# Four neighbouring rows of a down matrix on each partition, and eight passes of 64 columns in place of two transposes

## The chip, the core and the metric

The kernel runs on one core of a Trainium2 chip. The metric is the device time of one execution in microseconds (us); lower is better. Weights and activations are float32 and come from HBM through the core's 16 DMA engines into SBUF. TensorE (PE) multiplies into PSUM; its weight loads are shown as an engine of their own, PEld. ScalarE (ACT) and VectorE (DVE) read PSUM, SyncE (SP) issues nearly all transfers.

## What is computed

Two layers of a transformer trunk over 256 tokens of width 1024. Each layer has a mixture of three kinds of attention and then a mixture of 32 experts, of which every token takes two. The part that the change touches is the expert:

```python
def expert_block(args):
    xb, e = args
    h = jax.nn.silu(xb @ w_gate[e]) * (xb @ w_up[e])
    return h @ w_down[e]
```

`w_gate[e]` and `w_up[e]` are 1024 x 512, `w_down[e]` is 512 x 1024: 2 MB each in float32, so 6.29 MB for an expert and 403 MB for the 64 experts of both layers.

## The kernel before, in words

Each engine runs a program of its own, and semaphores join them. The experts' matrices come as chunks of 2 MB, always in the order gate, up, down, through a ring of eight slots in SBUF and, for two of the first chunks of a layer, through two extra places. SP issues a chunk as soon as its slot is free (L431 for gate and up, L429 for down); TensorE frees slots by raising a semaphore (L1570). While a layer's attention runs, the first ten chunks of its experts are fetched; then the DMA stands until TensorE frees the slots of the first expert. A layer has four rounds of eight experts.

An expert has at most 32 tokens in the regular pass, and on TensorE it takes these steps:

- `products` (L1521): the 32 gathered token columns times gate and up. The four halves (gate 0:256, gate 256:512, up 0:256, up 256:512) are computed side by side in four column tiles of 32 columns, so that `gu_ps` has four groups of 32 rows by 256 columns. ACT copies that to `h_rows`, and then TensorE frees the two slots.
- `turned` / `turns` (L1530 and L1532): `h_rows` is transposed back into `h_ps`, so that hidden units lie on the partitions. This is two transposes of 128 x 128 (L1530). Two more transposes (L1532) turn the gates and places of the tokens into `pgt_ps`.
- `neg_exp` on ACT (L668) and `hidden` on DVE (L1044 to L1047) make silu(gate) * up, which is `hid`.
- `down_of` (L1538): `hid` times the down chunk, in four column tiles of 32 columns, one for each `k` of the chunk.
- `add` (L1546): the result is scattered into the accumulators of all tokens.

The order on TensorE, for expert e, is products(e), down_of(e - 1), turned(e), add(e - 1). At the end of a round it is down_of(6), products(7), turned(7), add(6), down_of(7), add(7).

Which hidden unit sits on which partition is set twice, and the two must agree: by the view of the down matrix that SP loads (`down_v`), and by which columns of `h_rows` a transpose takes (`by_step`). Before, partition p holds units 2p, 2p + 1, 256 + 2p and 257 + 2p: two runs of two rows, 8 KB each.

Of the kernel before, what the change touches and what calls it, by code (L numbers as in the profile page):

```python
# [20 lines left out]
ALU = mybir.AluOpType  # L21
# [145 lines left out]
def trunk(nc, x_d, w_in, w_out, norm_mix, norm_ffn, rel_bias, lam_q1, lam_k1, lam_q2, lam_k2,  # L167
# [4 lines left out]
    with ctx:  # L172
# [14 lines left out]

        h_ps = pv[:, 1, 0:2 * P].rearrange("p (c h s) -> p c h s", c=HALF // P, h=4)
        pgt_ps = pv[:, 1, 2 * P:(2 + TOK) * P]
# [77 lines left out]

        hid = take(2 * P).rearrange("p (b c h s) -> p b c h s", b=2, c=HALF // P, h=2)
        e_neg = take(2 * P).rearrange("p (b c n) -> p b c n", b=2, c=HALF // P)
        sig = take(P).rearrange("p (c n) -> p c n", c=HALF // P)  # L270
        rlog = take(TOK * R_COLS).rearrange("p (t n) -> p t n", t=TOK)
# [14 lines left out]

        ident = con[:, C_ID:C_ID + P]

        xT_raw = rows.rearrange("p t f -> p (t f)").rearrange("p (j s) -> p j s", j=KD)
# [53 lines left out]
        up_v = w_up.rearrange("l e (p j) d -> (l e) p j d", j=KD)  # L343
        down_v = w_down.rearrange("l e (h p c) n -> (l e) p h c n", h=2, c=KE // 2)

# [4 lines left out]
        def down_chunk(flat):  # L350
            return flat.rearrange("p (k n) -> p k n", k=KE)

        def down_rows(flat):

            return flat.rearrange("p (h c n) -> p h c n", h=2, c=KE // 2)

# [32 lines left out]
        def _(sp):  # L389
# [6 lines left out]
            for l in range(DEPTH):  # L396
# [14 lines left out]
                for m in range(ROUNDS):  # L411
                    for c in (*range(6), *EXTRA, 6, 7, *range(EXTRA[-1] + 1, 3 * BODY)) if m == 0 else range(3 * BODY):
                        e = l * N_EXPERTS + m * BODY + c // 3
                        if m == 0 and c == 5:
                            sp.wait_ge(lg_done, at(l, NS, 8))
                            sp.dma_start(gain_ffn, bcast_row(norm_ffn, l, D_MODEL)).then_inc(gain_f_in, 16)
                        if m == 0 and c in EXTRA:
                            i = EXTRA.index(c)
                            sp.wait_ge(ssq_ready, l * RMS + 5)
                            if c % 3 == 2:  # L420
                                sp.dma_start(down_rows(extra[i]), down_v[e]).then_inc(extra_full[i], 16)
                            else:
                                sp.dma_start(extra[i].rearrange("p (j n) -> p j n", j=KD), (gate_v, up_v)[c % 3][e]
                                             ).then_inc(extra_full[i], 16)
                            continue
                        s, fill = place(m * 3 * BODY + c)
                        sp.wait_ge(slot_free[s], at(l, FILLS[s], fill))
                        if c % 3 == 2:
                            sp.dma_start(down_rows(ring[:, s, :]), down_v[e]).then_inc(slot_full[s], 16)  # L429
                        else:  # L430
                            sp.dma_start(chunk(s, 512), (gate_v, up_v)[c % 3][e]).then_inc(slot_full[s], 16)  # L431
                    if m == 0 and l + 1 < DEPTH:
                        load_small(sp, l + 1)
# [5 lines left out]
                with sp.If(more > 0):  # L439
                    with sp.Fori(0, more) as k:  # L440
                        i = done + k
                        e = sp.value_load(over_e_i[0:1, bass.ds(k, 1)], min_val=0, max_val=N_EXPERTS - 1)
                        for c, w in enumerate((gate_v, up_v, down_v)):
                            sp.wait_ge(slot_free[c], at(l, FILLS[c], FILLS[c] + 1))
                            sp.wait_ge(over_free, i + 1)
                            sp.sem_inc(passed["sp"], 1)
                            sp.dma_start(down_rows(ring[:, c, :]) if c == 2 else chunk(c, 512), w[l * N_EXPERTS + e]
                                         ).then_inc(over_full[c], 16)
# [59 lines left out]
        def _(act):  # L508
# [30 lines left out]
            for l in range(DEPTH):  # L539
# [127 lines left out]
                def neg_exp(b):  # L667
                    return nc.scalar.activation(e_neg[:, b], h_ps[:, :, 0:2, :].rearrange("p c h s -> p c (h s)"),  # L668
                                                ACT.Exp, scale=-1.0)
# [66 lines left out]
        def _(dve):  # L736
# [11 lines left out]
            for l in range(DEPTH):  # L748
# [292 lines left out]
                def hidden(b, ready, turned):  # L1041

                    gate, up = (h_ps[:, :, a:a + 2, :].rearrange("p c h s -> p c (h s)") for a in (0, 2))
                    own.link(v.tensor_scalar(sig, e_neg[:, b], 1.0, None, ALU.add))  # L1044
                    own.link(v.reciprocal(sig, sig))  # L1045
                    own.link(v.tensor_tensor(sig, gate, sig, ALU.mult))
                    v.tensor_tensor(hid[:, b].rearrange("p c h s -> p c (h s)"), up, sig, ALU.mult  # L1047
                                    ).then_inc(ready, 1)
# [106 lines left out]
        def _(pe):  # L1155
# [6 lines left out]
            for l in range(DEPTH):  # L1162
# [363 lines left out]
                def turns(i):  # L1526

                    by_step = h_rows.rearrange("q (p c) -> q c p", c=HALF // P)
                    for c in range(HALF // P):
                        turn_(h_ps[:, c].rearrange("p h s -> p (h s)"), by_step[:, c], ident)  # L1530
                    for t in range(TOK):
# [3 lines left out]
                def down(flat, b, half):  # L1535

                    for k in range(KE):
                        ins = mm(tr[k * CAP:(k + 1) * CAP, half], hid[:, b, k % 2, k // 2, :],  # L1538
                                 down_chunk(flat)[:, k, 512 * half:512 * half + 512],
# [163 lines left out]
```

## Time and profile before

| what | value |
|---|---|
| median of 3 runs | 1256.07 us (1255.79 to 1257.69) |
| the profiled execution | 1253.63 us |
| its span, first to last instruction | 1251.3 us |
| TensorE busy | 85% of the span |
| TensorE weight loads busy | 49% |
| VectorE, ScalarE, GpSimd busy | 28%, 19%, 2% |
| read from HBM | 441.59 MB, 354 GB/s over the span |
| mean granted TensorE clock | 0.927 |

The profile is of one execution. Busy shares are means over a span of very different stages: in two long stretches the DMA moves some 425 GB/s without a pause, and between them it does less than half of that. So the views by stage and the chain of work that ended last say more than the shares. A line number stands for a line of the kernel; a helper's line can stand for many calls. Matmuls are pipelined, so the start to start distance of neighbours says more than the duration of one.

### The profile page before, as it was taken

How to read it: one execution, taken by the hardware profiler on the slowest of the kernel's cores; microseconds unless marked ns; L12 is line 12 of the kernel's file. 1: busy time of each engine (PE TensorE's matmuls, PEld its weight loads, DVE VectorE, ACT ScalarE, POOL GpSimd, SP SyncE). 2: the span in 40 equal slices, each digit the busy share in tenths (PEclk: the TensorE clock that was granted, in tenths of full speed). 3: DMA queues.
4: the chain of work that ended last, by engine and by line, in shares of the span. 5: the costliest groups of instructions: out<-in, count | busy, mean ns of one | idle time of the engine just before them, and what ended most of it. 6: DMA issues, size and time to landing. Idle time of an engine off the chain costs nothing.

```text
span 1251.3 us, 18635 instructions
## 1 busy us (share of the span) xinstructions
PE 1060.1 (85%) x7940; PEld 608.6 (49%) x7940; DVE 345.5 (28%) x962; ACT 237.3 (19%) x574; POOL 18.8 (2%) x49
## 2 busy tenths in 40 slices
PE   8999999976877788777799999998787878696876
PEld 4877565443433344434358765554444344343532
DVE  3444562211211111111235364721111211111113
ACT  2234212201111111111112341121111111110111
POOL 1000100000000000000010000000000000000000
PEclk9999999987989888888999999999889888897989
DMA  7674549999999999999995144699999999999994
GB/s 259 247 305 172 212 150 426 425 359 426 427 425 421 425 426 425 426 425 426 412 387 210 53 176 178 257 428 426 425 425 426 424 425 423 426 425 427 425 424 181
DMA packets 63141, 443.89 MB, mean 355 GB/s; under 512 B 10409, under 2 KB 14929, under 8 KB 30289
## 3 DMA queue, kind: packets, MB, share of 16 engines
q1 hardware_dynamic: 61072, 440.94, 85.7%
q10 hardware_dynamic: 1984, 1.72, 0.4%
q8 instruction: 66, 1.08, 0.3%
q14 instruction: 19, 0.15, 0.0%
HBM read 441.59 MB, written 1.06 MB: 354 GB/s over the span
## 4 chain that ended last, share of the span: by engine, by line
DMA 46%; PE 44%; SPq 2%; ACT 2%; DVE 2%; issue 2%; PEld 1%; PEldq 0%; POOL 0%; POOLq 0%; ACTq 0%; DVEq 0%
DMA ring<-in_w_up 45%; PE pv L1521 14%; PE pj L1194 7%; PE pj L1200 4%; PE pj L1428 4%; PE tr L1538 3%; SPq L383 2%; PE pj L1546 2%; PE lg L1546 2%; ACT arena L511 1%; PE tr L1507 1%; PE lg L1229 1%; DMA ring<-in_w_in 1%; DMA bias<-bias_lines 1%; PE pv L1260 1%
## 5 line engine op out<-in xcount | busy, mean ns | idle before, releaser
L1521 PE MATMUL pv<-ring,xT 128*32 128x256 f32 x4032 | 298.4, 457 | 159.2 <-DMA ring<-in_w_up 159.1
L1521 PEld LDWEIGHTS pv<-ring,xT 128*32 128x32 f32 x4032 | 167.8, 131 | 292.2 <-issue 245.1
L1044 DVE TENSOR_SCALAR arena<-arena 128x128 f32<-128x128 f32 x64 | 14.5, 227 | 705.6 <-ACT arena L668 705.3
L1546 PE MATMUL pj<-arena 128*128 128x512 f32 x256 | 131.5, 596 | 0.0
L1546 PE MATMUL lg<-arena 128*128 128x512 f32 x256 | 130.8, 592 | 0.0
L511 ACT ACTIVATE arena<-pv 128x256 f32<-128x256 f32 x64 | 24.5, 383 | 542.2 <-PE pv L1521 542.2
L1538 PE MATMUL tr<-ring,arena 128*32 128x512 f32 x992 | 118.7, 594 | 0.0
L511 ACT ACTIVATE arena<-tr 128x512 f32<-128x512 f32 (+3 forms) x168 | 92.3, 558 | 126.8 <-PE tr L1538 106.5
L1194 PE MATMUL pj<-xT,ring 128*128 128x256 f32 (+1 forms) x480 | 107.9, 381 | 0.6 <-PE pj L1194 0.6
L1194 PEld LDWEIGHTS pj<-xT,ring 128*128 128x128 f32 (+1 forms) x480 | 87.3, 185 | 17.5 <-issue 2.7
L1546 PEld LDWEIGHTS lg<-arena 128*128 128x128 f32 x256 | 48.7, 190 | 61.2 <-issue 61.2
L1507 PEld LDWEIGHTS tr<-arena,rows 128*128 128x128 f32 x512 | 59.7, 192 | 7.0 <-issue 6.7
L1546 PEld LDWEIGHTS pj<-arena 128*128 128x128 f32 x256 | 43.7, 191 | 37.3 <-issue 37.3
L1045 DVE RECIPROCAL arena<-arena 128x128 f32<-128x128 f32 x64 | 61.0, 952 | 2.2
L1507 PE MATMUL tr<-arena,rows 128*128 128x128 f32 x512 | 59.7, 275 | 0.0
L1538 PEld LDWEIGHTS tr<-ring,arena 128*32 128x32 f32 x992 | 32.8, 110 | 54.9 <-issue 48.1
L1428 PE MATMUL pj<-ring,xT 128*128 128x512 f32 x128 | 57.4, 596 | 1.0 <-ACT xT L511 1.0
L1530 PEld LDWEIGHTS pv<-con,arena 128*128 128x128 f32 x128 | 20.2, 207 | 59.4 <-issue 59.4
L511 ACT ACTIVATE xT<-tr 128x512 f32<-128x512 f32 x36 | 21.3, 597 | 109.9 <-PE tr L1507 90.0
L1530 PE MATMUL pv<-con,arena 128*128 128x128 f32 x128 | 31.9, 331 | 11.9 <-ACT arena L511 11.9
L511 ACT ACTIVATE arena<-pj 64x256 f32<-64x256 f32 (+2 forms) x52 | 22.2, 428 | 77.0 <-PE pj L1194 63.9
L1428 PEld LDWEIGHTS pj<-ring,xT 128*128 128x128 f32 x128 | 23.4, 190 | 26.9 <-issue 26.9
(200 smaller groups left out, 753.4 us busy)
## 6 DMA issues: line engine op xcount, KB each, us to landing
ring<-in_w_up SPq DMA_DIRECT2D x64, 2048.0 KB, 21.8
ring<-in_w_gate SPq DMA_DIRECT2D x62, 2048.0 KB, 30.8
ring<-in_w_down SPq DMA_DIRECT2D x62, 2048.0 KB, 26.3
ring<-in_w_in SPq DMA_DIRECT2D x10, 2048.0 KB, 19.5
ring<-in_w_out SPq DMA_DIRECT2D x4, 2048.0 KB, 16.9
arena<-in_w_down SPq DMA_DIRECT2D x2, 2048.0 KB, 7.9
arena<-in_w_gate SPq DMA_DIRECT2D x2, 2048.0 KB, 12.3
ring<-in_w_in SPq DMA_DIRECT2D x2, 1760.0 KB, 14.4
```

What stands on the lines that cost most here:

```text
L383: eng.dma_start(dst, src).then_inc(small_in, 16)
L511: return nc.scalar.activation(out, in_, ACT.Copy, **k)
L1044: own.link(v.tensor_scalar(sig, e_neg[:, b], 1.0, None, ALU.add))
L1045: own.link(v.reciprocal(sig, sig))
L1194: ins = mm(out, w[:, j], xT[:, j, :], start=(j == 0), stop=(j == KD - 1))
L1200: ins = mm(out, src[:, j, t * P:(t + 1) * P], chunk(i, n)[:, j, c:c + m], start=(j == 0), stop=(j == KD - 1))
L1428: ins = mm(pj[:, half], xT[:, k, t * P:(t + 1) * P], chunk(6 + half, 512)[:, k, :], start=(k == 0), stop=(k == KD - 1))
L1507: ins = mm(wide_ps[:, j * n:(j + 1) * n], rows[:, t, j * P:(j + 1) * P], pick[:, t, 0:n], start=(t == 0), stop=(t == TOK - 1))
L1521: ins = mm(gu_ps[i * CAP:(i + 1) * CAP, :], xg[:, q, j, c:c + CAP], w[:, j, :], start=(j == 0), stop=(j == KD - 1), tile_position=(0, i * ...
L1530: turn_(h_ps[:, c].rearrange("p h s -> p (h s)"), by_step[:, c], ident)
L1538: ins = mm(tr[k * CAP:(k + 1) * CAP, half], hid[:, b, k % 2, k // 2, :], down_chunk(flat)[:, k, 512 * half:512 * half + 512], start=True, ...
L1546: ins = mm(acc[t][half], pgT[:, b, t, :], y[:, 512 * half:512 * half + 512], start=False, stop=last, skip_group_check=True)
```

## The change

The down chunk gets the layout that gate and up have: partition p holds the rows 4p to 4p + 3 of the matrix, 16 KB in one run. To match that, the halves of the hidden units go to halves of the partitions: units 0:256 to partitions 0 to 63, units 256:512 to partitions 64 to 127. `turns` takes every fourth column of `h_rows` (64 of them) as the stationary side and half of the identity's columns (64) as the moving side; with four steps `c` and two halves `h` there are eight passes, and the column tile (0, 64h) puts the result in the lower or upper partitions. They are ordinary float32 matmuls and no longer transposes. `neg_exp` and `hidden` read the new order, with as many elements as before.

```diff
-        h_ps = pv[:, 1, 0:2 * P].rearrange("p (c h s) -> p c h s", c=HALF // P, h=4)
+        h_ps = pv[:, 1, 0:2 * P].rearrange("p (c g s) -> p c g s", c=KE, g=2)
...
-        hid = take(2 * P).rearrange("p (b c h s) -> p b c h s", b=2, c=HALF // P, h=2)
+        hid = take(2 * P).rearrange("p (b c s) -> p b c s", b=2, c=KE)
...
+        ident_by_half = ident.rearrange("p (g h s) -> p g h s", g=2, h=2)
...
-        down_v = w_down.rearrange("l e (h p c) n -> (l e) p h c n", h=2, c=KE // 2)
+        down_v = w_down.rearrange("l e (p c) n -> (l e) p c n", c=KE)
...
-                            sp.dma_start(down_rows(ring[:, s, :]), down_v[e]).then_inc(slot_full[s], 16)
+                            sp.dma_start(down_chunk(ring[:, s, :]), down_v[e]).then_inc(slot_full[s], 16)
...
-                    return nc.scalar.activation(e_neg[:, b], h_ps[:, :, 0:2, :].rearrange("p c h s -> p c (h s)"),
+                    return nc.scalar.activation(e_neg[:, b], h_ps[:, :, 0, :],
                                                 ACT.Exp, scale=-1.0)
...
-                    gate, up = (h_ps[:, :, a:a + 2, :].rearrange("p c h s -> p c (h s)") for a in (0, 2))
+                    gate, up = h_ps[:, :, 0, :], h_ps[:, :, 1, :]
...
-                    by_step = h_rows.rearrange("q (p c) -> q c p", c=HALF // P)
-                    for c in range(HALF // P):
-                        turn_(h_ps[:, c].rearrange("p h s -> p (h s)"), by_step[:, c], ident)
+                    by_step = h_rows.rearrange("q (p c) -> q c p", c=KE)
+                    for c in range(KE):
+                        for h in range(2):
+                            mm(h_ps[64 * h:64 * h + 64, c], by_step[:, c], ident_by_half[:, :, h, :],
+                               start=True, stop=True, tile_position=(0, 64 * h), skip_group_check=True)
...
-                        ins = mm(tr[k * CAP:(k + 1) * CAP, half], hid[:, b, k % 2, k // 2, :],
+                        ins = mm(tr[k * CAP:(k + 1) * CAP, half], hid[:, b, k, :],
```

## Rows read from the trace of the kernel before

**Rows 1.** The page's first part: each engine's busy time, share of span, instructions.

```profile
PE 1060.1 (85%) x7940; PEld 608.6 (49%) x7940; DVE 345.5 (28%) x962; ACT 237.3 (19%) x574; POOL 18.8 (2%) x49
```

**Rows 2.** The page's chain that ended last, shares of the span by line.

```profile
DMA ring<-in_w_up 45%; PE pv L1521 14%; PE pj L1194 7%; PE pj L1200 4%; PE pj L1428 4%; PE tr L1538 3%; SPq L383 2%; PE pj L1546 2%; PE lg L1546 2%; ACT arena L511 1%; PE tr L1507 1%; PE lg L1229 1%; DMA ring<-in_w_in 1%; DMA bias<-bias_lines 1%; PE pv L1260 1%
```

**Rows 3.** Windows of both expert stages: length, engines, PE clock, DMA share, GB/s.

```profile
265.00:606.00 341.00, 260.07 (x2240) 137.63 (x2240) 54.02 (x125) 47.37 (x99) 0.00 (x0) 0.87 1.01 425
822.00:1216.00 394.00, 316.84 (x2738) 167.88 (x2741) 67.44 (x155) 58.43 (x122) 0.00 (x0) 0.89 1.01 425
```

**Rows 4.** The chain by time, layer 0 (start, us, what): transfers of up.

```profile
383.17 24.73 DMA ring<-in_w_up
...
415.57 23.40 DMA ring<-in_w_up
...
448.15 20.29 DMA ring<-in_w_up
...
476.41 21.58 DMA ring<-in_w_up
```

**Rows 5.** The same chain in layer 1.

```profile
909.06 20.47 DMA ring<-in_w_up
937.50 22.67 DMA ring<-in_w_up
```

**Rows 6.** DMA view, 377.95 to 380.80 us: packets, MB, share of 16 engines.

```profile
q1 hardware_dynamic: 144, 1.18, 99.2%
```

**Rows 7.** DMA view, 368.20 to 375.80 us; 16 of the packets are semaphore writes.

```profile
q1 hardware_dynamic: 208, 3.15, 97.6%
```

**Rows 8.** The DMA view of 265 to 606 us, all packets and the queue.

```profile
DMA packets 12891, 144.95 MB, mean 425 GB/s; under 512 B 1102, under 2 KB 1102, under 8 KB 1102
...
q1 hardware_dynamic: 12871, 144.64, 100.5%
```

**Rows 9.** The page's DMA queues: the one that brings instructions.

```profile
q8 instruction: 66, 1.08, 0.3%
```

**Rows 10.** Windows where the experts of layer 1 begin, columns as in rows 3.

```profile
798.00:802.00 4.00, 3.94 (x68) 2.14 (x66) 3.59 (x10) 0.60 (x1) 0.00 (x0) 1.00 0.02 6
802.00:806.00 4.00, 3.31 (x56) 2.15 (x60) 3.51 (x14) 0.66 (x2) 0.00 (x0) 1.00 0.65 188
```

**Rows 11.** Timeline of SP in the same place: start, us, engine, line, transfer.

```profile
802.51 0.33 SPq L431 DMA_DIRECT2D ring<-in_w_up  x1
...
809.48 0.33 SPq L431 DMA_DIRECT2D ring<-in_w_gate  x1
```

**Rows 12.** A window in layer 0, while the next layer's small tensors are loaded.

```profile
260.00:264.00 4.00, 4.00 (x16) 1.43 (x18) 3.31 (x8) 0.18 (x1) 0.00 (x0) 1.00 0.68 152
```

**Rows 13.** Timeline of the last expert of layer 1, after its products.

```profile
1234.80 0.29 DVE L1047 TENSOR_TENSOR arena<-pv,arena 128x128 f32<-128x128 f32 x1
...
1236.25 0.64 PE L1538 MATMUL tr<-ring,arena 128*32 128x512 f32 x4
```

**Rows 14.** Timeline of TensorE around the four transposes of one expert.

```profile
1219.99 0.50 PE L1530 MATMUL pv<-con,arena 128*128 128x128 f32 x2
1220.33 0.38 PE L1532 MATMUL pv<-con,arena 128*128 128x128 f32 x2
1220.55 0.59 PE L1546 MATMUL pj<-arena 128*128 128x512 f32 x1
```

**Rows 15.** Timeline of TensorE from a full-width matmul to column tiles of 32.

```profile
1223.55 0.59 PE L1546 MATMUL lg<-arena 128*128 128x512 f32 x1
1224.07 0.16 PEld L1538 LDWEIGHTS tr<-ring,arena 128*32 128x32 f32 x8 [0.76 <-issue]
```

**Rows 16.** Timeline of TensorE: sixteen matmuls of 64 columns in attention.

```profile
729.78 2.00 PE L1260 MATMUL pv<-arena 128*128 128x64 f32 x16
```

**Rows 17.** Timeline of TensorE: one expert's products at full clock.

```profile
1227.78 3.66 PE L1521 MATMUL pv<-ring,xT 128*32 128x256 f32 x64 [1.78 <-DMA ring<-in_w_up]
```

More of the change, by code:

```diff
@@ L266, in trunk @@
         pgT = take(2 * TOK * P).rearrange("p (b t s) -> p b t s", b=2, t=TOK)
-        hid = take(2 * P).rearrange("p (b c h s) -> p b c h s", b=2, c=HALF // P, h=2)
-        e_neg = take(2 * P).rearrange("p (b c n) -> p b c n", b=2, c=HALF // P)
-        sig = take(P).rearrange("p (c n) -> p c n", c=HALF // P)
+        hid = take(2 * P).rearrange("p (b c s) -> p b c s", b=2, c=KE)
+        e_neg = take(2 * P).rearrange("p (b c s) -> p b c s", b=2, c=KE)
+        sig = take(P).rearrange("p (c s) -> p c s", c=KE)
         rlog = take(TOK * R_COLS).rearrange("p (t n) -> p t n", t=TOK)
@@ L351, in down_chunk @@
             return flat.rearrange("p (k n) -> p k n", k=KE)
-        def down_rows(flat):
-            return flat.rearrange("p (h c n) -> p h c n", h=2, c=KE // 2)
         def nk(t):
@@ L420, in _ @@
                             if c % 3 == 2:
-                                sp.dma_start(down_rows(extra[i]), down_v[e]).then_inc(extra_full[i], 16)
+                                sp.dma_start(down_chunk(extra[i]), down_v[e]).then_inc(extra_full[i], 16)
                             else:
@@ L446, in _ @@
                             sp.sem_inc(passed["sp"], 1)
-                            sp.dma_start(down_rows(ring[:, c, :]) if c == 2 else chunk(c, 512), w[l * N_EXPERTS + e]
+                            sp.dma_start(down_chunk(ring[:, c, :]) if c == 2 else chunk(c, 512), w[l * N_EXPERTS + e]
                                          ).then_inc(over_full[c], 16)
@@ L1046, in hidden @@
                     own.link(v.tensor_tensor(sig, gate, sig, ALU.mult))
-                    v.tensor_tensor(hid[:, b].rearrange("p c h s -> p c (h s)"), up, sig, ALU.mult
+                    v.tensor_tensor(hid[:, b], up, sig, ALU.mult
                                     ).then_inc(ready, 1)
```

## The prediction, made before the changed kernel was run

> **What bounds the kernel now.** The busy shares point to TensorE, 85% busy [rows 1], but they are a mean over unlike stages. The chain of work that ended last gives 45% of the span to one transfer, that of the up chunks [rows 2]. The windows over the expert stages say why: the DMA is busy all the time (share 1.01) at 425 GB/s in both layers, while TensorE is busy for 260 of 341 us and for 317 of 394 us, at a mean granted clock below full [rows 3]. The chain in order of time shows the beat. Two experts lie between neighbouring pieces, and a piece ends when its up chunk has landed: 407.90, 438.97, 468.44 and 497.99 us [rows 4]. The usual distance is 29.5 us, 14.76 us an expert, in which TensorE stands 3 us (77 us over 26.7 experts in layer 1, 81 over 23.1 in layer 0 [rows 3]). So inside these stretches only what the DMA does counts. A layer's stretch begins when TensorE frees its first slots and ends when the last up chunk has landed. Then the end is TensorE's own: turned(7), add(6), down_of(7), add(7).
>
> **Part 1: the down chunk in runs of 16 KB.** A window that holds only down packets has 144 of 8 KB; 99.2% of 16 engines for 2.85 us is 45.2 us, 314 ns each [rows 6]. A window with only gate and up has 192 packets of 16 KB and 16 semaphore writes; 97.6% of 16 engines for 7.6 us is 118.7 us, 617 ns each [rows 7]. The long stretch agrees: 144.64 MB in 11,769 large packets means 5,887 of 16 KB and 5,882 of 8 KB, and 1.005 x 16 x 341 us over them is 931 ns for one of each [rows 8]. So 16 KB cost 628 ns in two pieces and 617 in one. These durations overlap a little: 16 of either kind for each engine and expert make 14.90 us where the beat is 14.76, so each packet hides about 4 ns, and the gain of a joined pair is 7 to 11 ns. With 8 pairs for each engine and chunk, a down chunk gets 0.055 to 0.09 us shorter. I take 0.07. Which chunks count? In layer 1 the DMA stands at 798 to 802 us (share 0.02) [rows 10] and restarts with the up chunk of expert 3, issued at 802.51 [rows 11]. From there to the last up chunk, that of expert 31, the down chunks of experts 3 to 30 pass: 28. Layer 0 has the same order. 2 x 28 x 0.07 = 3.9 us gained (bounds 3.1 to 5.0; nothing, if the fixed part of a packet is paid elsewhere).
>
> **A page that gives less.** The Trainium skill, page "DMA: Bandwidth & Descriptors", section "Why small descriptors are slow (HBM only)", gives each packet about 3 beats of 32 bytes and each operation 32 bytes of metadata. By that one 8 KB packet fewer would save 4 of some 520 beats, 0.8% of 628 ns, an estimate of 5 ns; the gain would be about 2.2 us in place of 3.9. The rows show 7 to 11 ns, so I keep them.
>
> **Part 2: the small loads in layer 0.** Between 260 and 264 us the DMA is busy only 0.68 of the time, because SP has been issuing the next layer's small tensors [rows 12]; 1.3 us are empty. A down chunk with half as many descriptors may let SP get through sooner, or not. Bounds 0 and 1.3 us gained; I take 0.3.
>
> **Part 3: the turns on TensorE.** Before, two transposes and two more follow one another at about 0.11 us: from 1220.33 to 1220.55 is one such pair, and the first pair needs 0.34 from its start because the array comes from tiles of 32 columns [rows 14]. So the pair that goes is worth 0.22 us. What comes is eight float32 matmuls. The trace shows a float32 matmul as two weight loads and two matmuls (64 records at L1521 for the 32 calls of one expert [rows 17]) and a transpose as one (two for two calls [rows 14]), so it is 16 pairs of 64 columns. No row has such a tile. The nearest: sixteen full-width matmuls of 64 columns take 2.00 us, 0.111 from start to start [rows 16], held by weight loads of 128 columns; with loads of 64 columns half of that, 0.056. Tiles side by side do run together: 64 pairs over four tiles take 3.66 us, 0.057 each [rows 17], where 256 columns alone need twice the 0.11 of 128. With both halves together the 16 pairs need 8 x 0.056 = 0.45 us, one after another 0.9, and with load and matmul also one after another 1.8. Then comes a change from tiles of 64 to full width, ahead of the L1532 transposes, that was not there. Such a change costs about 0.1 us in two rows: 0.34 in place of 0.22 above, and a matmul of 512 columns that starts at 1223.55 and streams for four times 0.11 is done at 1223.98, while the next load starts at 1224.07 [rows 15]. The Trainium skill, page "TensorEngine Tiling (Array Packing)", section "Key Properties", says that a change of the tiling mode drains the array; the rows agree with their 0.1 us. Together: 0.45 + 0.15 (a little more, for the load behind it) - 0.22 = +0.4 us for each expert; bounds +0.2 and +1.8. I take the low side since rows 17 show tiles that overlap.
>
> Where does it count? Inside the stretches it lies under the 3 us for which TensorE waits for the DMA; without that cover it would be 64 x 0.4 = 26 us. At the end of each layer it counts in full: turned(7) is followed by add(6) and down_of(7), and those wait for nothing else. DVE has `hid` ready at 1235.1 and down_of(7) starts at 1236.25 [rows 13], so the activation chain has 1.1 us to spare, also for a slower strided read of PSUM. 2 x 0.4 = 0.8 us lost (0.4 to 3.6). At a layer's beginning each expert's turns delay the later slots. Up and down are issued at 802.5, flow from about 803.4 (share 0.65 in 802 to 806 [rows 10]) and last 9.8 us, to 813.2; the next issue is at 809.48 [rows 11], and the first data come 0.9 us after an issue. That leaves 2.8 us for two turns. At +0.4 each nothing is lost.
>
> **Part 4: instructions.** Each expert gets 28 more of them, 1,792 in all. The instruction queue moved 66 packets of 16 KB for 18,635 instructions [rows 9], 58 bytes each, so some 6 more packets on the same 16 engines. They matter since a chunk has landed only when the last engine has finished. The beat does show steps: 31.07 us where 29.5 is usual [rows 4], and from 929.53 to 960.17 us 30.64 [rows 5]; there are two of each kind in the stretches, and with smaller ones they sum to 6 us. If instruction packets cause them, a tenth more is +0.6 us, and since they would fall elsewhere, anything from -2 to +3.
>
> **Sum.** -3.9 - 0.3 + 0.8 + 0.6 = -2.8 us. The profiled execution (span 1251.3, device time 1253.63) would become 1250.8. It was 2.4 us below the median of the runs, and the sum is carried over to that median: 1256.07 - 2.8 = 1253.3 us.
>
> **The rivals.** (A) The gain of a packet is not there or is only the 5 ns of the page. Against it stand rows 6 to 8; for it, that durations are not throughput, and 4 ns of each overlap already. Then the time is 1256.07 + 0.8 + 0.6 - 0 to 2.2, 1255.3 to 1257.5 us. (B) The gain is at its upper bound (5.0), the hole at 260 us closes (1.3) and no new step comes in the beat: 1256.07 - 5.0 - 1.3 + 0.8 = 1250.6 us. (C) Slower: the 16 passes do not flow. If each pair waits for the one before it, with two tiles side by side, a pass costs a weight load and a matmul in full: 0.27 us (two at L1532 last 0.38 and start 0.11 apart [rows 14]) and some 0.13 (eight small loads are done in 0.16 [rows 15]); eight of them are 3.2, +3.1 for each expert. The ends of the layers lose 6.2, the beginnings 2 x (2 x 3.1 - 2.8) = 6.8, and TensorE's 3 us of spare in an expert are just used up: 1256.07 - 4.2 + 0.6 + 13.0 = 1265.5 us. It decides from about +2 us for each expert, where 2 x 2 + 2 x (2 x 2 - 2.8) has overtaken 3.6 us and the 2.5 of the border. Rows 16 and 17 speak against it, for they show loads that run under matmuls.
>
> **How the numbers follow.** Forecast 0.55, at 1253.3 with its own range 1251.5 to 1255; A 0.20, B 0.17, C 0.08. A measurement of this kernel can tell about 0.2% from no change, so 1253.6 and 1258.6 are the borders. The forecast lies just inside: 0.31 of its 0.55 are faster and 0.24 the same. With B that is 0.48 faster; with A 0.44 the same; C is the 0.08 slower. The range for 8 in 10 leaves out C and half of the ends of A and B: 1249.9 to 1257.2.
>
> **What would show it.** The usual distance of neighbouring chain pieces falls from 29.50 to 29.36 us. A window of down packets shows 16 KB packets of 617 ns, and the long stretch 426 to 427 GB/s. The start of L1530 to that of L1532 grows from 0.34 to 0.75 us. From the last up chunk's landing to the last L1546, each layer's end grows by 0.4 us. TensorE waits less for the up chunks. The prediction is wrong if the distance stays at 29.5 (A), if the turns take over 2 us (C), or if the steps in the beat change in number by more than one in a layer.

## The result and the profile after

The changed kernel takes 1263.25 us (median of 5 runs, 1262.13 to 1263.65) against 1256.07: ratio 1.0053, 95% interval 1.0037 to 1.0069. Ratios in this text are taken over the fast runs of both kernels and are not exactly those of the two medians. It is slower by half a per cent, where 1253.3 was predicted and 1257.2 was the upper end of the range. The profiled execution took 1262.13 us, its span is 1260.2, 8.9 longer than before.

The page after: engines, the queue that brings instructions, the group of the products (busy us, mean ns, idle before and what ended it).

```profile
PE 1097.4 (87%) x8836; PEld 650.9 (52%) x8836; DVE 346.2 (27%) x962; ACT 237.5 (19%) x574; POOL 18.9 (1%) x49
...
q8 instruction: 73, 1.20, 0.4%
...
L1518 PE MATMUL pv<-ring,xT 128*32 128x256 f32 x4032 | 279.1, 434 | 125.0 <-DMA ring<-in_w_up 124.9
```

Beside [rows 1] TensorE has 896 matmuls more and is busy for 37 us more. That is not where the time went: the wait of the products for the up chunks fell (it was 159.1 us, at L1521 of the kernel before), since the longer turns lie in it. Lines of the changed kernel stand 1 to 3 lower: its products are L1518, the turns L1528, the transposes of the gates L1531, down L1537, scatter L1545.

The transfers did what was forecast. Pieces of the chain in layer 0 (start, length), and the window to compare with [rows 3]:

```profile
419.13 21.25 DMA ring<-in_w_up
449.19 20.68 DMA ring<-in_w_up
477.60 21.69 DMA ring<-in_w_up
```

```profile
265.00:606.00 341.00, 275.42 (x2569) 153.64 (x2572) 55.54 (x128) 48.00 (x100) 0.00 (x0) 0.91 1.01 426
```

The pieces end at 440.38, 469.87 and 499.29 us: 29.49 and 29.42 apart where [rows 4] have 29.47 and 29.55, and the rate is 426 instead of 425 GB/s. In the landings of single chunks it is plainer: apart from a few steps, all three kinds now come 4.893 us apart, where a down chunk took 4.965 before, 0.07 more.

The turns, in the timeline of TensorE of the last expert:

```profile
1240.29 1.18 PE L1528 MATMUL pv<-con,arena 128*64 128x64 f32 x16 [0.74 <-ACT arena L508]
1241.39 0.44 PE L1531 MATMUL pv<-con,arena 128*128 128x128 f32 x2
```

From the first pass to the first transpose of the gates it is 1.10 us, where [rows 14] have 0.34, and the scatter starts 1.38 after the first pass instead of 0.56: +0.82 us per expert.

The largest piece is one that nobody had looked for. The chain from the end of layer 0 into layer 1 (start, length, what), and the windows over the same place:

```profile
618.33 3.69 PE pv L1518 x64
...
632.34 0.86 PE lg L1545 x2
633.20 5.13 issue
638.33 1.89 PE tr L1263 x4
640.22 1.71 PE tr L1271 x8
641.92 1.71 PE pv L1271 x8
643.63 5.55 PE pj L1197 x16
```

```profile
633.00:638.00 5.00, 0.20 (x1) 0.00 (x0) 0.76 (x2) 2.19 (x4) 1.79 (x6) 0.88 1.05 387
638.00:642.00 4.00, 3.67 (x14) 2.65 (x15) 0.73 (x2) 0.00 (x0) 0.00 (x0) 0.50 1.06 388
```

"Issue" is time in which TensorE waited for nothing that the profile shows: 5.13 us. After it the granted clock stands at 0.50, its level of 1.2 GHz, and four short matmuls that took 0.86 us before take 1.89. From the last scatter of layer 0 to the first piece of 16 matmuls of layer 1 (L1197, the attention's projections) it is 10.43 us (633.20 to 643.63); before it was 2.85 (631.64 to 634.49). That is 7.6 us, and as that first piece is 0.17 shorter, 7.4.

So the span's +8.9 us is put together like this: the program's start +2.8 (its first 16 matmuls took 8.70 us, most of it at half clock, instead of 5.75; kernels with the turns of before show both, see below), expert stretch of layer 0, from its first products to the landing of its last up chunk, -2.1, turns at its end +0.85, the gap and the slow clock behind it +7.4, stretch of layer 1 -0.9, turns at its end +0.8.

### The profile page after: what moved, and what is told of

Its sections match the earlier page's. It is cut to its first block, busy times and chain, and to the rows that moved or that the text cites. A ratio compares the mean times of both kernels' runs of the same rounds, so it can differ in the third digit from the quotient of the medians.

```text
span 1260.2 us, 20427 instructions
## 1 busy us (share of the span) xinstructions
PE 1097.4 (87%) x8836; PEld 650.9 (52%) x8836; DVE 346.2 (27%) x962; ACT 237.5 (19%) x574; POOL 18.9 (1%) x49
## 4 chain that ended last, share of the span: by engine, by line
PE 46%; DMA 43%; issue 3%; SPq 2%; DVE 2%; PEld 2%; ACT 2%; PEldq 0%; POOL 0%; POOLq 0%; ACTq 0%
DMA ring<-in_w_up 42%; PE pv L1518 14%; PE pj L1191 8%; PE pj L1197 4%; PE pj L1425 4%; PE pj L1545 2%; PE lg L1545 2%; PE tr L1537 2%; SPq L380 2%; PEld pv L1528 1%; PE pv L1528 1%; PE tr L1504 1%; PE lg L1226 1%; ACT arena L508 1%; DMA ring<-in_w_in 1%
## 5 line engine op out<-in xcount | busy, mean ns | idle before, releaser
L1518 PE MATMUL pv<-ring,xT 128*32 128x256 f32 x4032 | 279.1, 434 | 125.0 <-DMA ring<-in_w_up 124.9
L1518 PEld LDWEIGHTS pv<-ring,xT 128*32 128x32 f32 x4032 | 158.7, 124 | 247.1 <-issue 194.3
L1545 PE MATMUL pj<-arena 128*128 128x512 f32 x256 | 131.5, 595 | 0.0
L1545 PE MATMUL lg<-arena 128*128 128x512 f32 x256 | 130.7, 592 | 0.0
L1537 PE MATMUL tr<-ring,arena 128*32 128x512 f32 x992 | 118.7, 594 | 0.0
L1528 PEld LDWEIGHTS pv<-con,arena 128*64 128x64 f32 x1024 | 66.9, 214 | 59.4 <-issue 59.4
L1528 PE MATMUL pv<-con,arena 128*64 128x64 f32 x1024 | 75.2, 288 | 11.9 <-ACT arena L508 11.9
L1545 PEld LDWEIGHTS lg<-arena 128*128 128x128 f32 x256 | 48.6, 190 | 61.2 <-issue 61.2
L1545 PEld LDWEIGHTS pj<-arena 128*128 128x128 f32 x256 | 43.6, 190 | 37.3 <-issue 37.3
L1537 PEld LDWEIGHTS tr<-ring,arena 128*32 128x32 f32 x992 | 32.9, 110 | 54.9 <-issue 48.1
```

Source lines behind the costliest of these rows:

```text
L1518: ins = mm(gu_ps[i * CAP:(i + 1) * CAP, :], xg[:, q, j, c:c + CAP], w[:, j, :], start=(j == 0), stop=(j == KD - 1), tile_position=(0, i * ...
L1528: mm(h_ps[64 * h:64 * h + 64, c], by_step[:, c], ident_by_half[:, :, h, :], start=True, stop=True, tile_position=(0, 64 * h), skip_group_c ...
L1537: ins = mm(tr[k * CAP:(k + 1) * CAP, half], hid[:, b, k, :], down_chunk(flat)[:, k, 512 * half:512 * half + 512], start=True, stop=True, t ...
L1545: ins = mm(acc[t][half], pgT[:, b, t, :], y[:, 512 * half:512 * half + 512], start=False, stop=last, skip_group_check=True)
```

## Experiments

The ratios are to the kernel before on the same chip (1254.2 to 1255.0 us). A ratio of 0.001 is 1.25 us.

**Where does the gap come from?** It stands where the work of layer 1 begins, right behind a jump over the overflow pass (the code for experts with more than 32 tokens), which TensorE never enters with these inputs. TensorE's built program has 16,986 instructions before and 18,834 after; the instruction queue moved 66 and 73 packets of 16 KB for it [rows 9]. That is 256 instructions a packet (16,986 / 256 = 66.4, 18,834 / 256 = 73.6), so the program can be counted in blocks of 256. Before, the jump lands 0.35 into block 33, with 166 instructions left in it. After, it lands 0.96 into block 36, with 10 left. (Behind the same jump in layer 1 the program ends.) The theory: behind the jump the next block has first to be fetched, and with only 10 instructions left TensorE runs dry. The DMA view of 635.50 to 636.50 us of the changed kernel, where TensorE stands since 633.20, has such a packet:

```profile
q8 instruction: 1, 0.02, 6.6%
```

TensorE goes on at 638.33. Ahead of that packet, from 623.20 to 635.60, that queue brings none, so the next block is not there when TensorE lands. The rivals to the theory: the longer body that is jumped over (289 instead of 261 instructions) costs the time, or the faster chunks do.

*The kernel before, moved to a bad place.* Semaphore increments that nobody waits for, 13 behind the products of 12 experts in layer 0 (156), and nothing else; the jump lands 0.96 into its block, with 10 instructions left as in the changed kernel.

```diff
                         products(e)
+                        if l == 0 and m in (1, 2):
+                            for _ in range(13):
+                                pe.sem_inc(filler, 1)
                         down_of(e - 1)
```

> The kernel before with 156 more instructions on TensorE (13 for each of 12 experts of layer 0, as in e6_after_shift) and nothing of the change. Now its jump lands 10 instructions before the end of a block, as in the changed kernel. Position theory: a piece of about 5 us of issue at the start of layer 1 and a half clock behind it, 1256.1 + 7.4 = 1263.5 us. Rivals (longer body; timing of the turns; something in the 16 KB transfers): none of these is in this kernel, so 1256 to 1257 us.

Measured: 1261.26 us, ratio 1.0055 (1.0039 to 1.0072), so +6.9 us (4.9 to 9.0) for increments that do no work. Its chain at the same place:

```profile
634.24 4.40 issue
638.64 1.04 PE tr L1267 x4
639.68 1.61 PE tr L1275 x8
641.29 1.71 PE pv L1275 x8
642.99 5.58 PE pj L1201 x16
```

The gap is there without anything of the change: 8.75 us from the last scatter to the first piece of 16 matmuls instead of 2.85. That is 5.9 us; of the rest of its span's +8.5 us, 2.6 are a slow start of this one execution (first 16 matmuls 8.42 us).

*The changed kernel, moved to good places.* The same lines, once with 8 increments per expert (96; the jump lands 0.33 into a block), once with 13 (156; 0.57).

> The changed kernel with 96 more instructions on TensorE (semaphore increments that nobody waits for, 8 for each of 12 experts of rounds 1 and 2 of layer 0, where TensorE waits for the DMA anyway). Position theory: TensorE's program comes in blocks of 256 instructions (16 KB of 64 bytes; 73 packets on the instruction queue for some 18,800 instructions). In the changed kernel the jump over the overflow pass at the end of layer 0 lands 10 instructions before the end of a block, so the next block is needed before it is there: that is the 5.1 us of issue at 633.20 us, and the half clock behind it another 2.3 us. 96 more instructions put the landing in the middle of a block: no such piece, 1263.3 - 7.4 = 1255.9 us. Rival (the skipped body is longer than a block and grew by 56 instructions): body unchanged, stall unchanged, 1263 to 1264 us. Rival (the later turns set TensorE's and the DMA's timing at the end of the layer): unchanged, 1263 to 1264.

> The changed kernel with 156 instead of 96 increments that nobody waits for, so that the jump lands elsewhere in a block, again far from its end (at 0.57 of the block instead of 0.33). Theory of the block's end: as with 96, no issue gap, ratio to before 1.001 to 1.004 (the layout's gain 0.9977 and the price of the passes without a gap, 1.0035 to 1.007). Rival (the place in the block isn't what counts, 96 was luck): the gap is back, ratio 1.005 to 1.007. At the layers' last products the clock theory expects 5.4 us at one end or both with a chance of one half, a loss of 1.7 us each.

Measured: 1256.04 us, ratio 1.0013 (0.9998 to 1.0028), and 1255.39 us, ratio 1.0005 (0.9996 to 1.0014). Neither has the gap. Their chains, first with 96, then with 156:

```profile
634.57 0.86 PE tr L1264 x4
635.43 0.45 PE tr L1272 x4
...
637.42 5.72 PE pj L1198 x16
```

```profile
635.24 0.86 PE tr L1264 x4
636.10 0.45 PE tr L1272 x4
636.65 1.30 DVE rows L756 x2
638.09 5.72 PE pj L1198 x16
```

From 634.57 to 637.42 and from 635.24 to 638.09 it is 2.85 us each, as before. So the place of the landing in its block decides. It is far from the end in three kernels without a gap (0.33, 0.35, 0.57), 10 instructions before it in two with one. Against the changed kernel, 96 or 156 idle instructions more save 0.40 and 0.48% (5.0 and 6.0 us, each known to some 2 us).

With 156 increments TensorE is at the landing at 635.24, and the next packet comes no sooner than in the kernel with the gap: the queue brings none from 624.30 to 637.80, and from 637.80 to 639.05

```profile
q8 instruction: 1, 0.02, 5.5%
```

So the block behind is fetched late in either kernel; what differs is whether 110 instructions or 10 are left to work on until it comes.

*Only the body that is jumped over is longer* (the kernel before with 28 more instructions in the overflow pass of each layer, 289 instead of 261; lands at 0.46).

```diff
+                    for c in range(2):
+                        mm(h_ps[:, c].rearrange("p h s -> p (h s)"), h_rows.rearrange("q (p c) -> q c p", c=2)[:, c], ident, start=True, stop=True)
+                    for c in range(6):
+                        mm(h_ps[:, c % 2].rearrange("p h s -> p (h s)"), h_rows.rearrange("q (p c) -> q c p", c=2)[:, c % 2], ident, start=True, stop=True)
...
-                        turns(0).then_inc(o_h, 1)
+                        turns_long().then_inc(o_h, 1)
```

> The kernel before with a longer overflow pass: as many instructions as in the changed kernel (56 more in the skipped body of each layer). These inputs never enter it. Body theory (the jump over a longer body makes TensorE's next instructions late): 1263 us, with the issue piece at the start of layer 1. Position theory: the landing moves by 56 instructions from 33.35 to 33.57 blocks, far from a block's end, so no piece and 1256 us.

Measured: 1255.06 us, ratio 1.0004 (0.9994 to 1.0015), no gap. (The landing of layer 0 moves by the 28 instructions of one body, not by 56.) The body's length is not it.

*Landing 38 instructions before the end* (the changed kernel, its overflow pass with two transposes in place of the eight passes).

```diff
+                    for c in range(2):
+                        turn_(pv[:, 1, c * P:(c + 1) * P], h_rows[:, c * P:(c + 1) * P], ident)
...
-                        turns(0).then_inc(o_h, 1)
+                        turns_short().then_inc(o_h, 1)
```

> The changed kernel with the turns of the overflow pass cut from eight passes to two whole transposes (the overflow pass, which would compute wrong values with it, is never entered with these inputs). The jump over it starts at the same place and lands 28 instructions earlier: 38 instead of 10 before the end of the block. Theory of the block's end: the gap comes 28 instructions later in TensorE's stream, behind most of the turns of the first product rows, and what was issued before hides part of it: 1 to 4 us under the changed kernel, gap shorter or at a later line. Rival (the jump's length or the body's instructions cost the time): 28 of 288 instructions fewer change less than 0.5 us, the gap stays 5 us at the same line.

Measured: 1262.61 us (1260.56 to 1264.42), ratio 1.0060 (1.0045 to 1.0075): no shorter than the changed kernel, so the 1 to 4 us did not come. The place did move as the theory has it:

```profile
634.79 0.86 PE tr L1263 x4
635.66 4.25 issue
639.91 1.97 PE tr L1271 x8
641.88 1.51 PE pv L1271 x8
643.38 5.48 PE pj L1197 x16
```

TensorE gets four matmuls further before it stands, and the gap ends only 1.6 us later than in the changed kernel; the stage takes 8.59 us instead of 10.43. The 1.8 us gained here are in this profile lost again at the layers' ends (below). What can be said: 38 instructions are too few, 110 (the landing at 0.57) are enough; nothing in between was tried.

**What is each half of the change worth?** *The layout alone*: the down rows as in the change, the turns as before (of the program only the two lines of `down_v` and the chunk's view differ).

```diff
-        down_v = w_down.rearrange("l e (h p c) n -> (l e) p h c n", h=2, c=KE // 2)
+        down_v = w_down.rearrange("l e (p c) n -> (l e) p c n", c=KE)
...
-            return flat.rearrange("p (h c n) -> p h c n", h=2, c=KE // 2)
+            return flat.rearrange("p (k n) -> p k n", k=KE)
```

> The kernel before with the new place of the down rows in their chunk (a partition holds four neighbouring rows, one run of 16 KB) and nothing else: two transposes per expert as before, and TensorE's instructions in number and order those of before. The rows of the down matrix and the hidden units then don't match, so the output isn't the reference's; the work is the same. Price of the transfers by the prediction: 56 down chunks x 0.07 us = 3.9 us off. Theory of the sum by parts (the gain is all there and the loss comes from the passes and from TensorE's program): 3 to 4 us under before, ratio 0.997, chunks landing 4.89 us apart throughout. Rival (the chunks' gain is mostly eaten by steps in the landings, so that the new layout is worth little by itself): within 1.5 us of before, ratio 0.999 to 1.000.

Measured: 1250.68 us, ratio 0.9977 (0.9967 to 0.9988): 2.9 us faster (1.5 to 4.1). In its chain the last up chunk of layer 0 lands at 614.99 us, 2.5 earlier than before, and that of layer 1 at 1223.17, 4.5 earlier. The forecast for this part was 3.9 + 0.3. Of the 4.5 us, 0.4 lie ahead of the experts. The stretches alone, from a layer's first products to its last up chunk, shorten by 2.1 us in layer 0 (436.7 to 434.6) and by 2.0 in layer 1 (429.3 to 427.3), 4.0 together. The chain in layer 1, before and with the layout alone:

```profile
798.35 3.63 PE pv L1521 x64
...
1206.62 21.02 DMA ring<-in_w_up
```

```profile
795.86 3.63 PE pv L1521 x64
...
1202.40 20.77 DMA ring<-in_w_up
```

*The passes alone* (old layout), at their unlucky place and, with the 96 increments, at a lucky one.

```diff
-                    by_step = h_rows.rearrange("q (p c) -> q c p", c=HALF // P)
-                    for c in range(HALF // P):
-                        turn_(h_ps[:, c].rearrange("p h s -> p (h s)"), by_step[:, c], ident)
+                    by_step = h_rows.rearrange("q (p c) -> q c p", c=KE)
+                    for c in range(KE):
+                        for h in range(2):
+                            mm(h_ps[64 * h:64 * h + 64, c], by_step[:, c], ident_by_half[:, :, h, :],
+                               start=True, stop=True, tile_position=(0, 64 * h), skip_group_check=True)
```

> The kernel before with the eight passes of 64 columns and the rows of the hidden values that go with them, but the old place of the down rows (two runs of 8 KB per partition). Again rows of the down matrix and hidden units don't match, the work is the same; TensorE's program has the same instructions at the same places as the changed kernel. Theory of the jump near a block's end (the passes' 1,792 further instructions move the jump over the overflow pass to 10 instructions before the end of a block of 256): an issue gap of 4 to 5 us before the first turn of layer 1, then half clock, together about 7 us in the profile (5 us in the medians); with turns of +0.8 us at two layer ends the median comes 7 to 9 us above before, ratio 1.006 to 1.007. Rival (the gap in the changed kernel came out of the new layout's faster chunks): no gap, 1 to 2 us above before, ratio 1.001.

> The last kernel (eight passes, old place of the down rows) with 96 semaphore increments that nobody waits for, 8 behind the products of each of 12 experts of layer 0, so that the jump lands far from a block's end. Rows of the down matrix and hidden units don't match. It prices the passes without the gap. Theory of the sum by parts: two layer ends x 0.83 us = 1.7 us above before, ratio 1.0013, no issue gap at the start of layer 1. Rival (the passes cost more than at the ends: the difference of the shifted changed kernel, 1.0013, and of the layout's gain, 0.997, is 4 to 5 us): 4 to 5 us above before, ratio 1.0035 to 1.004, with the rest to be found as slower clock at the layer ends or as late chunks.

Measured: 1265.79 us, ratio 1.0096 (1.0081 to 1.0110), with a gap of 5.25 us; and 1262.01 us, ratio 1.0069 (1.0050 to 1.0089), without. Moving the landing saves 3.8 us here. The gap comes with the instructions, not with the layout. But both kernels are slower than expected, and the second shows by how much the sum by parts falls short: 8.7 us (6.3 to 11.2) where two layer ends give 1.7. Its chain at the ends of layers 0 and 1:

```profile
618.37 5.38 PE pv L1522 x64
...
624.46 1.17 PE pv L1532 x16
```

```profile
1232.18 5.51 PE pv L1522 x64
```

The products of the last expert take 5.38 and 5.51 us instead of 3.69: the mean granted clock over them is 0.68, TensorE is at 1.2 GHz for most of them. That is 1.7 and 1.8 us on the path, since a layer's last expert has nothing that hides it. With 1.7 for the passes and 0.75 and 1.1 us by which the stretches of layers 0 and 1 last longer, it makes the 7.0 us by which its span is longer.

**Is it the time of the turns or the passes themselves?** The two transposes of before, issued four times over: as many columns (8 x 128) as in the passes (16 x 64). 156 increments keep the landing in the middle of a block (0.50).

```diff
-                    for c in range(HALF // P):
-                        turn_(h_ps[:, c].rearrange("p h s -> p (h s)"), by_step[:, c], ident)
+                    for c in range(4 * (HALF // P)):
+                        turn_(h_ps[:, c % 2].rearrange("p h s -> p (h s)"), by_step[:, c % 2], ident)
```

> The kernel before, old place of the down rows, with its two transposes of 128 columns of each product row issued four times over (eight transposes; the output is that of the reference): as many columns through TensorE as in the eight passes of 64 columns, 1,024, without tiles of 64 columns. 156 semaphore increments that nobody waits for in layer 0 let the jump over the overflow pass land in the middle of a block. Turns by the transposes' 0.12 us apiece: about +0.7 us per expert, so +1.4 us at two layer ends. Theory (more time and columns in the turns shift the clock's falls onto the layers' last products, which then take 5.4 instead of 3.7 us, in some executions): like the shifted kernel with the passes, 5 to 8 us above before, ratio 1.004 to 1.007, and 5.4 us at a layer's end in the profile with a chance of one half. Rival (that comes with the tiles of 64 columns or with the further instructions): 1.4 us above before, ratio 1.001, both ends at 3.7 us.

Measured: 1257.58 us, ratio 1.0021 (1.0012 to 1.0030), +2.6 us (1.5 to 3.8): between the two theories' numbers, nearer to the rival's 1.4. In its profile the turns cost 0.7 us at each end, and the stretch of layer 1 is 2.1 us longer than before (431.4 instead of 429.3), for which no run here shows the reason. Both ends are at full clock:

```profile
620.01 3.69 PE pv L1522 x64
...
624.41 1.20 PE pv L1531 x8
```

```profile
1232.95 3.69 PE pv L1522 x64
```

Over all profiles: in the six kernels without the passes (before, longer body, before moved, layout alone, four times over, and the next one) the last products of both layers ran at 2.4 GHz, twelve ends of twelve. In the six with the passes they ran at half clock for most of their time in both layers in four (changed kernel with 96 and with 156, short body, passes alone moved) and at full in two (changed kernel, passes alone). The passes as such don't bring the slow clock, then. What sorts the ends better is how long TensorE stood for the up chunk just before. It stood for 2.51 to 2.63 us at ten ends, all in kernels with the passes, and eight of them are slow; the two others are those of the changed kernel. It stood for 0.3 to 2.2 us at the other fourteen (the twelve without the passes, and 0.81 and 1.14 us in the passes alone), and none is slow. Layer 0 before, in the changed kernel (full clock) and with 96 increments (slow), the idle time in brackets:

```profile
617.63 0.64 PE L1521 MATMUL pv<-ring,xT 128*32 128x256 f32 x8 [2.19 <-DMA ring<-in_w_up]
```

```profile
618.33 0.64 PE L1518 MATMUL pv<-ring,xT 128*32 128x256 f32 x8 [2.53 <-DMA ring<-in_w_up]
```

```profile
618.02 0.64 PE L1519 MATMUL pv<-ring,xT 128*32 128x256 f32 x8 [2.55 <-DMA ring<-in_w_up]
```

As there is one profile of each kernel, with what chance the slow ends come is not known, and no run sets the length of that wait on purpose, so the cause stays open. In the changed kernel with 156 increments the engine is busy for 0.14 us between 616 and 618, and then (length, PE, PEld, DVE, ACT, POOL, clock, DMA share, GB/s):

```profile
618.00:620.00 2.00, 1.32 (x22) 0.95 (x26) 0.00 (x0) 0.00 (x0) 0.00 (x0) 0.90 1.01 405
620.00:622.00 2.00, 2.00 (x24) 1.26 (x20) 0.00 (x0) 0.00 (x0) 0.00 (x0) 0.50 1.03 402
```

The changed kernel itself stood just as idle from 616 to 618 and kept its clock at 1.00. It need not be a constant cost either: that profile with both ends slow is of a run of 1258.7 us, the slowest of eleven with a median of 1255.39.

**A version that keeps the gain.** The layout of the change, but the columns that a transpose needs together are put together by the products: each matmul of a product takes its 256 columns as pairs, and the two transposes of 128 stay. No instruction is added.

```diff
-                    halves = [flat.rearrange("p (j n) -> p j n", j=KD)[:, :, h:h + HALF]
-                              for flat in (gate, up) for h in (0, HALF)]
+                    halves = [flat.rearrange("p (j m g c) -> p j g m c", j=KD, g=2, c=2)[:, :, g]
+                              for flat in (gate, up) for g in range(2)]
...
-                            ins = mm(gu_ps[i * CAP:(i + 1) * CAP, :], xg[:, q, j, c:c + CAP], w[:, j, :],
+                            ins = mm(gu_ps[i * CAP:(i + 1) * CAP, :].rearrange("q (m c) -> q m c", c=2), xg[:, q, j, c:c + CAP], w[:, j],
```

> The 16 KB layout of the down chunk without the eight passes: the products take the columns in pairs (units 4m, 4m + 1 in one column tile, 4m + 2, 4m + 3 in the other; the moving side reads 8 bytes out of 16), and two transposes bring them to partition m as before. As many instructions as before, so the jump lands where it did. Theory: the DMA's gain of 0.07 us for each down chunk stays (2.9 to 3.9 us), the ends of the layers cost nothing: 1252.2 to 1253.2 us, ratio 0.997 to 0.998. Rival: the read in pairs slows the products (3.66 us at full clock); at half speed an expert needs 15.5 us on TensorE, more than the DMA's 14.7, and the time is about 1300 us.

Measured: 1251.06 us, ratio 0.9975 (0.9965 to 0.9984), faster than both kernels. At the layers' ends the products take 3.92 and 3.87 us instead of 3.69, at full clock, which costs 0.4 of what the transfers give.

```profile
617.42 3.92 PE pv L1521 x62
...
622.05 0.48 PE pv L1530 x2
622.52 0.22 PE pv L1532 x2
```

## Why the prediction was wrong, point by point

The measured time lies above the range, and the loss has the other sign than the sum. Part 4 is the step that failed; the parts in us:

| | forecast | measured in the runs | in the profiles |
|---|---|---|---|
| layout (parts 1 and 2) | -4.2 | -2.9 (-4.1 to -1.5) | -4.0, stretches of the layout alone |
| turns at two layer ends (part 3) | +0.8 | not alone | +1.65 |
| instructions as load on the DMA (part 4) | +0.6 | not alone | +1.1, stretches of the changed kernel beside those of the layout alone |
| where the jump lands (in no part) | 0 | +6.9 (4.9 to 9.0) in the kernel before; 5.0, 6.0 and 3.8 where it is taken out | +7.4 |
| the program's start (in no part) | 0 | not alone | +2.8, of this execution |
| whole | -2.8 | +6.7 (4.6 to 8.7) | +8.9 |

The column of the profiles adds up. In the runs the passes with their instructions and without the gap cost +3.5 and +4.5 us (the changed kernel with 156 and with 96, less the layout alone), and +8.7 (6.3 to 11.2) on the old layout. The profiles of all three show a slow clock at both layers' ends (3.4 to 3.5 us together); in how many of their other runs it stands is not known.

- **What bounds the kernel**: right. The chain is still that of the up chunks within the layers, and the large costs that came stand outside them, at the layers' ends.
- **Part 1**: right. 0.07 us per down chunk was forecast and found, and the layout alone is 2.9 us faster in the runs, 4.0 in the stretches of its profile. The lower gain, the prediction's estimate of 2.2 us from the Trainium skill (page "DMA: Bandwidth & Descriptors", section "Why small descriptors are slow (HBM only)"), isn't excluded by the interval of the runs. The 0.07 us of the chunks speak against it: 5 ns for 8 pairs would be 0.04, and the measured 0.072 us are 9 ns a pair.
- **Part 2** (0.3): not told apart from part 1; too small to matter.
- **Part 3**: the place right, the size wrong. The passes take +0.82 us and not +0.4, inside the bounds (+0.2 to +1.8). The term that was too small is the 0.45 us for the sixteen pairs, which put two tiles side by side at 0.056 a pair since their weight loads have 64 columns. In the single records of the last expert the first and the last of the sixteen matmuls start 0.89 us apart (1240.286 and 1241.179), and the first transpose of the gates 0.21 later. From the second pair on, two starts lie 0.034 us apart and the next two 0.120 after them: 0.060 a matmul. So "0.9 one after another" was the right value, and the change back to full width cost about the 0.15 that the sum had for it (0.21 less the 0.06 of a matmul). Whether the two tiles ran side by side at 0.12 each or took turns at 0.06, the records don't tell. Within the stretches the 3 us hid the turns, as forecast: the products' wait fell. At the beginning of layer 1 the chain stays on TensorE, turns included, until 884.45 us, where before it passed to the up chunks at 850.65; as the DMA has a busy share of at least 1.00 all the while in both, nothing is lost there, as forecast.
- **Part 4** is the step that failed. It counted the 1,792 instructions and their packets and priced them only as load on the DMA engines (+0.6, bounds -2 to +3). That price was of the right size: beside the layout alone, the stretches of both layers together last 1.1 us longer in the changed kernel and 1.2 and 1.5 in its two moved versions, most of it in layer 1 (whether the packets do it is not shown; the four transposes lose 2.1 there). What it did not ask was where instructions are *missing* when TensorE wants them. It also divided the 66 packets by the 18,635 executed instructions of all engines, 58 bytes each; by the 16,986 of TensorE's program it is 64 bytes, and 256 instructions a packet. 28 more per expert moved the jump's landing from the first half of a block to 10 instructions before its end, and the engine stood for 5.13 us and then ran at half clock, 7.4 us in all. The number of further instructions was in the prediction, and the kernel has only one place in the middle of the program where TensorE jumps over some 280 instructions; both could have been put together, though the trace of before shows no such gap from which to price it.
- **The clock** at the layers' ends was left at full, as in all rows of before. It fell to half in four of the six profiles with the passes, 1.7 us an end, though not in that of the changed kernel. No term of the sum stands for that.
- **The base**: the profiled execution of before had its first 16 matmuls in 5.75 us. Of the other kernels without the passes, the pairs took 7.44, the moved one 8.42 and the four transposes 8.60, the layout alone and the longer body 5.75; and of the six with the passes five took 8.49 to 8.75 and one 5.75. So a slow start is found with either kind of turns, and whether the change makes it more frequent is not known; one profile of each kernel can't tell. The forecast laid a difference on the median and had no term for it.
- **The rivals**: none came. A and B differ only in the layout's gain. C forecast 1265.5 and comes nearest in time, but by another mechanism: it needed turns of over +2 us, and they are +0.82; that it comes near is luck. The range ended at 1257.2 because its only slower case had a chance of 0.08; a case "more instructions, at another place" was missing.

## What to carry to other kernels

Where an edit adds or removes instructions on an engine that jumps, count where the jump lands: a few idle instructions more or less ahead of it are then a cheap experiment, and a comparison of two versions is only fair when neither lands short of a block's end. Here 156 idle increments made the kernel before as slow as the change did, and took the loss out of the change. And look for the layout's gain without its price: rearranging what an existing matmul reads cost 0.2 us at a layer's end where new passes cost 0.8.

## What was not expected of the hardware

- TensorE's instructions arrive in packets of 16 KB, one for 256 instructions (66, 67, 73 and 74 packets for 16,986, 17,142, 18,834 and 18,930). After a jump that lands 10 instructions before a block's end the engine stood 4.4 to 5.25 us in three kernels, 4.25 after four more matmuls with 38 left, and not at all in eight profiles with 110 to 170 left.
- The gap is followed by half clock: the first four matmuls take 1.04 to 1.89 us, which are 0.86 at full clock, and the next eight 1.6 to 2.0, of which four take 0.45 at full clock.
- Sixteen matmuls of 64 columns on two column tiles of 64 start over 0.89 us, 0.060 apart in the mean. Sixteen full-width ones of 64 columns start 0.111 apart [rows 16]; the smaller weight loads and the two tiles together halved that and not more.
- Matmuls whose 256 moving columns are read in pairs, two apart, take 3.9 us for 64 where a plain read takes 3.7, both at full clock.
